# Moving the first five modulation slots behind the first feed-forward layer, and a buffer of its own for one key slot

## The reference, cut to what matters

```python
for i in range(2):                                   # first_block
    x = layer_norm(ALPHA * x + 0.5 * swiglu(x, ffn1...[i]), ...)
    y = mixer_ab(x, ...) if i % 2 == 0 else mixer_c(x, ...)
    x = layer_norm(ALPHA * x + y, ...)
    x = layer_norm(ALPHA * x + 0.5 * swiglu(x, ffn2...[i]), ...)
    x = x + sigmoid(x @ ple_wg[i] + ple_bg[i]) * (p[i] @ ple_wp[i])
for i in range(2):                                   # second_block
    sh1, sc1, g1, sh2, sc2, g2 = split(silu(c) @ w_ada[i] + b_ada[i], 6)   # the modulation
    h = x * (1 + sc1) + sh1
    y, yc = _even_mixer(h, hc, ...) if i % 2 == 0 else _odd_mixer(h, hc, ...)
    x = _layer_norm(ALPHA * x + g1 * y, ...)
    ...
```

## Time and profile before

| what | value |
|---|---|
| median of 3 runs | 2320.36 us (2312.47, 2320.36, 2321.82) |
| profiled execution, its own time | 2311.51 us |
| its span in the profile | 2310.2 us, 39754 instructions |
| mean granted clock of TensorE | 0.991 |
| DVE, ACT busy | 56%, 48% |
| DMA over the span | 353.63 MB, mean 153 GB/s |
| chain that ended last | PE 87%, DVE 6%, ACT 3%, DMA 2%, issue 1% |

### The profile page before, as it was taken

The page is one execution under the profiler, slowest core; times in us unless marked ns, Lnnn a source line. Parts: engine busy times, 40 slices in busy tenths (PEclk is TensorE's granted clock), DMA queues, the critical chain, the costliest instruction groups (busy, mean ns, idle before and its releaser), DMA issues.

```text
span 2310.2 us, 39754 instructions
## 1 busy us (share of the span) xinstructions
PE 2211.9 (96%) x17214; PEld 2003.0 (87%) x17214; DVE 1293.1 (56%) x1953; ACT 1103.0 (48%) x1740; POOL 54.2 (2%) x100
## 2 busy tenths in 40 slices
PE   6999989999999999999999989999999999999998
PEld 5999869999999899979998767888888886778998
DVE  3555756556555766465547326664444564676666
ACT  3444545445544554355445627553333454465554
POOL 1000100000000010010000000000000000000000
PEclk9999999999999999999999999999999999999999
DMA  8444645554545554456453211022222443304451
GB/s 326 183 166 171 259 182 220 186 191 165 190 175 192 205 216 169 159 196 248 166 199 110 91 73 38 20 92 92 91 91 108 166 146 116 122 10 173 170 195 56
DMA packets 52063, 353.63 MB, mean 153 GB/s; under 512 B 8112, under 2 KB 8496, under 8 KB 9392
## 3 DMA queue, kind: packets, MB, share of 16 engines
q1 hardware_dynamic: 47952, 346.05, 39.9%
q10 hardware_dynamic: 864, 4.63, 0.5%
q0 software_dynamic: 3072, 0.40, 0.1%
HBM read 349.61 MB, written 1.05 MB: 152 GB/s over the span
## 4 chain that ended last, share of the span: by engine, by line
PE 87%; DVE 6%; ACT 3%; DMA 2%; issue 1%; SPq 0%; ACTq 0%; DVEq 0%
PE ps L797 14%; PE ps L798 13%; PE ps L799 13%; PE ps L2579 5%; PE ps L2581 5%; PE ps L2580 5%; PE ps L410 2%; PE ps L411 2%; PE ps L412 2%; PE ps L944 2%; PE ps L2332 2%; PE ps L2334 2%; PE ps L2333 2%; DMA ring<-wstream 2%; PE ps L1559 2%; PE ps L1002 1%
## 5 line engine op out<-in xcount | busy, mean ns | idle before, releaser
L385 DVE TENSOR_TENSOR wl<-ring,wh 128x1024 fp32r<-128x1024 f32 x406 | 478.4, 1222 | 274.2 <-ACT wh L380 273.9
L797 PE MATMUL ps<-xs,wh 128*128 128x256 f32 x1760 | 501.4, 285 | 21.7 <-DVE wl L385 8.3
L798 PE MATMUL ps<-xs,wl 128*128 128x256 f32 x1760 | 500.1, 284 | 0.0
L799 PE MATMUL ps<-xs,wh 128*128 128x256 f32 x1760 | 500.0, 284 | 0.0
L380 ACT ACTIVATE wh<-ring 128x1024 fp32r<-128x1024 f32 x406 | 406.1, 1050 | 183.4 <-PE ps L799 128.1
L797 PEld LDWEIGHTS ps<-xs,wh 128*128 128x128 f32 x1760 | 339.9, 193 | 25.5 <-issue 20.5
L799 PEld LDWEIGHTS ps<-xs,wh 128*128 128x128 f32 x1760 | 339.9, 193 | 0.0
L798 PEld LDWEIGHTS ps<-xs,wl 128*128 128x128 f32 x1760 | 339.9, 193 | 0.0
L797 PE MATMUL ps<-hh,wh 128*128 128x256 f32 x880 | 249.1, 283 | 0.7 <-DVE hl L907 0.7
L798 PE MATMUL ps<-hh,wl 128*128 128x256 f32 x880 | 249.0, 283 | 0.0
L799 PE MATMUL ps<-hl,wh 128*128 128x256 f32 x880 | 249.0, 283 | 0.0
(11 more groups left out here) (467 smaller groups left out, 4130.5 us busy)
## 6 DMA issues: line engine op xcount, KB each, us to landing
ring<-wstream SPq DMA_DIRECT2D x329, 1024.0 KB, 4.9
ada_rows<-ada_stage POOLq DMA_DIRECT2D x96, 4.0 KB, 4.8
CN<-consts ACTq DMA_DIRECT2D x1, 1136.0 KB, 15.6
X<-xin ACTq DMA_DIRECT2D x1, 1024.0 KB, 10.6
X<-cin ACTq DMA_DIRECT2D x1, 1024.0 KB, 8.9
out<-X SPq DMA_DIRECT2D x4, 256.0 KB, 2.5
PT__65<-pin ACTq DMA_DIRECT2D x1, 512.0 KB, 18.7
ab_w<-wab ACTq DMA_DIRECT2D x1, 512.0 KB, 3.5
```

Of the source, the lines that this page charges most:

```text
L385: dve.tensor_tensor(lo, tile_of(i), hi.bitcast(F32), ALU.subtract).then_inc(low_part, 1)
L797: pe.matmul(out, wh[:, w, c, :], x_hi, start=start, stop=False, skip_group_check=True)
L798: pe.matmul(out, wl[:, w, c, :], x_hi, start=False, stop=False, skip_group_check=True)
L799: return pe.matmul(out, wh[:, w, c, :], x_lo, start=False, stop=True, skip_group_check=True)
```

## The change

The ada slots' total stays 48. The five at the start go: the stream begins with the first feed-forward layer. One more comes after the last slot of ab_out (TensorE makes it after tile 6), three more into the z tiles of mixer c (after tiles 24, 26 and 28) and one more after c_out's tile 6. All totals of `act_ada` follow. X is loaded by four DMAs of two rows of tiles each, ahead of PV; CN and `pin` are loaded, and `cond` is made, inside the first feed-forward layer after its second hidden tile. The two scaled biases move there too. In the even mixer slot 6 gets a high buffer of its own (`e_wh6`, 8 KB in scratch space), slot 8 waits for slot 4 only, ACT splits slots 7 and 8 together after key tile 1, TensorE puts one rotation behind each of the tiles of slots 5 and 6 but the last, and DVE makes the low parts of 7 and 8 ahead of the last rotation's arithmetic.

```diff
-SECTIONS = ([("ada", 5), ("ffn1_0", 33), ("ada", 1), ("ab_in", 1), ("ada", 3)] + [("ab_in", 1), ("ada", 1)] * 4
-            + [("ab_in", 2), ("alibi", 2)] + [("ab_out", 1), ("ada", 1)] * 4 + [("ffn2_0", 33), ("ple_p_0", 1)]
+SECTIONS = ([("ffn1_0", 33), ("ada", 1), ("ab_in", 1), ("ada", 3)] + [("ab_in", 1), ("ada", 1)] * 4
+            + [("ab_in", 2), ("alibi", 2)] + [("ab_out", 1), ("ada", 1)] * 3 + [("ab_out", 1), ("ada", 2)] + [("ffn2_0", 33), ("ple_p_0", 1)]
...
-            + [x for name, n in (("c_k", 3), ("c_v", 4), ("c_q", 4), ("c_z", 4)) for x in [(name, 1), ("ada", 1)] * n]
-            + [("c_out", 2), ("ada", 3)] + [("c_out", 1), ("ada", 1)] * 2 + [("ada", 1), ("ffn2_1", 33), ("ple_p_1", 1), ("ple_g_1", 4)]
+            + [x for name, n in (("c_k", 3), ("c_v", 4), ("c_q", 4)) for x in [(name, 1), ("ada", 1)] * n]
+            + [("c_z", 1), ("ada", 2)] * 3 + [("c_z", 1), ("ada", 1)]
+            + [("c_out", 2), ("ada", 3)] + [("c_out", 1), ("ada", 1)] * 2 + [("ada", 2), ("ffn2_1", 33), ("ple_p_1", 1), ("ple_g_1", 4)]
...
@@ act_ffn
-                act_xhigh(src)
+                for q in range(4):
+                    c = slice(2 * q, 2 * q + 2)
+                    act.wait_ge(in_x[q], 16)
+                    act.activation(xs[:, c, 0, :], src[:, c, :], ACT.Copy).then_inc(x_high, 1)
...
+                if f == 0 and t == 1:
+                    act.dma_start(CN[:, :], consts).then_inc(in_consts, 16)
+                    act.dma_start(PT_[:, :, :, :], pin).then_inc(in_p, 16)
+                    act.wait_ge(in_params, 16)
+                    act.activation(cond[:, :, :, :], pcol("cond", 0, 16).rearrange("p (c j) -> p c j", j=2).unsqueeze(2)
+                                   .broadcast_to([P, KC, 16, 2]), ACT.Silu).then_inc(cond_ready, 1)
@@ dve_ffn
             if f == 0:
+                for q in range(4):
+                    dve.wait_ge(in_x[q], 16)
                 dve_xlow(name, src)
...
+                if beside and t == 1:
+                    beside()
@@ pe_mixer_ab
-                if n in (1, 3, 5):
+                if n in (1, 3, 5, 6):
                     pe_ada(8)
@@ pe_mixer_c
             tile(24)
+            pe_ada(8)
...
             tile(26)
+            pe_ada(8)
...
             tile(28)
+            pe_ada(8)
...
-                if t in (3, 5):
+                if t in (3, 5, 6):
                     pe_ada(8)
@@ the even mixer
+        e_wh6 = put("e_wh6", [SLOT], F32R, ("hsc", 4096))
...
         def slot_high(s):
-            return e_wh0[:, :] if s == 0 else (e_wh if s < 11 else e_wh2)[:, (s + 1) % 2, :]
+            if s in (0, 6):
+                return (e_wh0 if s == 0 else e_wh6)[:, :]
+            return (e_wh if s < 11 else e_wh2)[:, (s + 1) % 2, :]
...
-            elif s >= 2:
-                before, k = E_SLOTS[s - 2]
+            elif s >= 2 and s != 6:
+                before, k = E_SLOTS[4 if s == 8 else s - 2]
...
+            rotated(0)
+            rotated(1)
...
+            for t in range(4):
                 pe.wait_ge(*e_out.at(f"qB{t}"))
-                pe_slot_tile(6, t % 2, t, hi, lo)
+                pe_slot_tile(5 + t // 2, t % 2, t, hi, lo)
+                if t < 3:
+                    rotated(2 + t)
...
                 act.activation(e_kB[:, t, :], ps[:, t, :], ACT.Copy).then_inc(*e_out(f"kB{t}"))
-                if t % 2:
-                    act_slot_high(7 + t // 2)
+                if t == 1:
+                    act_slot_high(7)
+                    act_slot_high(8)
...
                 if t == 2:
                     dve_slot_low(6)
+                elif t == 4:
+                    dve_slot_low(7)
+                    dve_slot_low(8)
...
-            dve_slot_low(7)
-            dve_slot_low(8)
@@ pe_program, act_program, dve_program
-            pe_ada(40)
-            pe.wait_ge(in_x, 16)
-            pe.wait_ge(in_consts, 16)
-            pe.wait_ge(in_p, 16)
...
                 pe_ffn(2 * i, f"ffn1_{i}")
+                if i == 0:
+                    pe.wait_ge(in_consts, 16)
+                    pe.wait_ge(in_p, 16)
...
-            for s, dst, src in ((in_params, PV[:, :], params), (in_x, X[:, 0, :, :], xin), (in_consts, CN[:, :], consts),
-                                (in_p, PT_[:, :, :, :], pin)):
-                act.dma_start(dst, src).then_inc(s, 16)
...
-            act_ada(40)
-            act.wait_ge(in_x, 16)
+            for q in range(4):
+                act.dma_start(X[:, 0, 2 * q:2 * q + 2, :], xin[:, 2 * q:2 * q + 2, :]).then_inc(in_x[q], 16)
+            act.dma_start(PV[:, :], params).then_inc(in_params, 16)
...
```

More of the change, by code:

```diff
@@ L831, in pe_ffn @@
             gate_up(1)
-            pe.wait_ge(ada_copied, ada["mm"] // KC)
+            if ada["mm"]:
+                pe.wait_ge(ada_copied, ada["mm"] // KC)
             down(0)
@@ L886, in act_ffn, with dve_ffn @@
                     residual(t - 2)
-        def dve_ffn(f, name, src, coef, conv=None, ahead=0, after=()):
+                if f == 0 and t == 1:
[4 more added lines that the diff above has]
+                                   .broadcast_to([P, KC, 16, 2]), ACT.Silu).then_inc(cond_ready, 1)
+        def dve_ffn(f, name, src, coef, conv=None, ahead=0, after=(), beside=None):
             i0 = TILE0[name]
             if f == 0:
+                for q in range(4):
+                    dve.wait_ge(in_x[q], 16)
                 dve_xlow(name, src)
@@ L1980, in act_mixer_c @@
             act_high(t0 + 29)
-            act_ada(296)
+            act_ada(272)
             z_tile(2)
+            act_ada(280)
             act_high(t0 + 30)
@@ L1985, in act_mixer_c @@
             act_high(t0 + 31)
-            act_ada(304)
+            act_ada(288)
             z_tile(4)
+            act_ada(296)
             act.wait_ge(c_att_p, 2)
@@ L2413, in pe_even_mixer, with rotated @@
                 pe_slot_tile(3 + t // 2, t % 2, t, hi, lo)
-            for t in range(5):
+            def rotated(t):
                 q = e_qA[:, t, 0:T] if t < 4 else e_kA[:, 0:T]
@@ L3198, in act_program @@
         def act_program():
-            for s, dst, src in ((in_params, PV[:, :], params), (in_x, X[:, 0, :, :], xin), (in_consts, CN[:, :], consts),
-                                (in_p, PT_[:, :, :, :], pin)):
-                act.dma_start(dst, src).then_inc(s, 16)
-            act.wait_ge(in_params, 16)
-            act.activation(cond[:, :, :, :], pcol("cond", 0, 16).rearrange("p (c j) -> p c j", j=2).unsqueeze(2)
-                           .broadcast_to([P, KC, 16, 2]), ACT.Silu).then_inc(cond_ready, 1)
-            act_ada(40)
-            act.wait_ge(in_x, 16)
+            for q in range(4):
+                act.dma_start(X[:, 0, 2 * q:2 * q + 2, :], xin[:, 2 * q:2 * q + 2, :]).then_inc(in_x[q], 16)
+            act.dma_start(PV[:, :], params).then_inc(in_params, 16)
             act_ffn(0, "ffn1_0", X[:, 0], after=tiles("ab_in"))
             act.wait_ge(eps_set, 3)
-            act_layer_norm("ffn1_0", 64)
+            act_layer_norm("ffn1_0", 24)
             act_mixer_ab()
-            act_layer_norm("ab", 152)
+            act_layer_norm("ab", 120)
             act_ffn(1, "ffn2_0", None, ahead=2, after=tiles("ple_g_0"))
@@ L3214, in act_program @@
             act_ple(0)
-            act_ffn(2, "ffn1_1", X[:, 0], ahead=4, copies=168, after=tiles("c_k"))
-            act_layer_norm("ffn1_1", 192)
+            act_ffn(2, "ffn1_1", X[:, 0], ahead=4, copies=136, after=tiles("c_k"))
+            act_layer_norm("ffn1_1", 160)
             act_mixer_c()
@@ L3241, in dve_program, with scaled_biases @@
             dve.memset(ln_eps[:, 1:2], 1e-6).then_inc(eps_set, 1)
-            dve.wait_ge(in_params, 16)
-            for k, (name, at) in enumerate(LN_AB.values()):
-                dve.tensor_scalar(ln_eps[:, at:at + KC], pcol(LN_GB[name][1], 0, KC), ALPHA, None, ALU.mult
-                                  ).then_inc(eps_set, 1)
-            for s in (in_x, in_consts):
-                dve.wait_ge(s, 16)
+            def scaled_biases():
+                dve.wait_ge(in_params, 16)
+                for name, at in LN_AB.values():
+                    dve.tensor_scalar(ln_eps[:, at:at + KC], pcol(LN_GB[name][1], 0, KC), ALPHA, None, ALU.mult
+                                      ).then_inc(eps_set, 1)
             half = lambda c: 0.5
-            dve_ffn(0, "ffn1_0", X[:, 0], half, after=tiles("ab_in"))
+            dve_ffn(0, "ffn1_0", X[:, 0], half, after=tiles("ab_in"), beside=scaled_biases)
+            dve.wait_ge(in_consts, 16)
             dve_norm_to_parts("ffn1_0")
```

68 lines of the change are left out of this document (33 added, 35 removed).

## The result

| what | before | after |
|---|---|---|
| median of 7 runs each, on one chip | 2315.46 us | 2301.41 us (2298.34 to 2306.78) |
| ratio of the times, 95% interval | | 0.9941 (0.9929 to 0.9953) |
| profiled execution, its own time | 2311.51 us | 2299.87 us |
| its span | 2310.2 us | 2298.6 us |
| mean granted clock of TensorE | 0.991 | 0.993 |

The change makes the kernel faster by 0.59%: 0.0059 x 2315.46 = 13.7 us, with the interval from 10.9 to 16.4. The two profiled executions differ by 11.6. The forecast was 12.7 less, or 2304 us. The prediction took 0.5% for the least that a measurement of this kernel can tell. The interval, 0.47% to 0.71%, reaches across that: the new kernel is faster than the one before, but not clearly by more than 0.5%.

A forecast was written before the change was run, and what follows sets the result against it. TensorE was taken as the bound, its matmuls filling 96% of the span. The terms -10.3 + 0.5 + 5.0 + 1.0 - 8.9 gave -12.7 us, from the runs' mean 2316.5 to 2304; the range ran from 2292 less 2 up to 2313.

The forecast's parts named there:

- Start: Kernel's head: without five ada slots, X is in at 15.5 us and TensorE starts at 20.7 instead of 31.00, -10.3 us.
- turns by packets: Loads at the start: DMA queues alternate by packets, not bytes, so 512 packets of X go beside 512 of the stream.
- slow packets: Rival at the start, chance 0.05: small packets slow the stream to 380 GB/s or below; at most -11.4 us, 2305.
- Clock: First matmuls: TensorE, having done nothing before, runs slow somewhat longer; +0.5 us, between no further loss and 0.9.
- Five ada slots: New places in ab_out, z tiles and c_out: each costs 1.00 us of TensorE, +5.0 us (bounds +3.0 and +8).
- Stream around the layer norms: Behind ab_out and c_out: the next layer's second slot lands later and delays the layer norm, +0.5 us each, +1.0.
- Stream in the z tiles: Mixer c: the changed ring order makes slots z2 and z3 load later, but cover remains, so it costs nothing.
- rival on the slow side: Z tiles and layer norms behind ab_out and c_out: loads land after 10 us instead of 4.9; +12.7 us, 2329, chance 0.06.
- Even mixer: Product with slots 7 and 8: stop gone (-4.8), slow matmuls behind it (-3.0), bunched rotations (-1.1); -8.9 us in all.
- come back in the attention: Rival, chance 0.13: the even mixer's gain is lost again to the attention's first step or the clock; -3.8 us, 2312.7.

The follow-up runs named there:

- e2: The changed kernel without the even mixer's part, so only the new start and the five moved ada slots: 2309.52 us, ratio 0.9984 to the kernel before.
- e5: The changed kernel with one matmul of 8 columns in each of the five moved ada slots: 2298.21 us, ratio 0.9930 to the kernel before.
- e8: The changed kernel with the stream's third slot held until X is in: 2295.20 us, ratio 0.9921 to the kernel before.
- e3: The changed kernel with X loaded by one DMA (8 KB packets) instead of four: 2294.63 us, ratio 0.9914 to the kernel before.
- e7: The changed kernel with slot 8 split behind key tile 3 again and its low part last: 2314.47 us in one execution.
- e1: The kernel before with only the even mixer's part of the change, start and ada slots as before: 2306.98 us, ratio 0.9967 to the kernel before.
- e6: The changed kernel with three rotations together behind key tile 1 and the low parts of slots 7 and 8 last: 2302.38 us in one execution.
- e9: The changed kernel with X in one DMA and the first two weight tiles' splitting put between X's parts: 2291.58 us, ratio 0.9901 to the kernel before.

## Why the prediction came out as it did

- **Start, -10.3 forecast, -8.95 measured.** The mechanism was right at each link: turns by packets (477 and 476), X beside the stream, DVE's 5.04 us behind it. But X was in at 17.0, not 15.5, and two terms of that sum were mis-sized. The rate of 0.42 MB/us held only from 6.5 us on (420 GB/s); the 3.5 us before that had 323, which is 0.34 MB or 0.8 us. And from 3 to 17 us not 5.24 MB went by but 5.54: 4.42 of the stream and 1.12 on X's queue, where the first packets of PV had begun before the last of X were in. That is the other 0.7 us. The rival "slow packets" gave nearly this landing (16.8) and had 0.05, but its mechanism did not come: 2 KB packets beside 8 KB ones kept up 420 GB/s, not 380. Its closeness is chance. Why the first 3.5 us are slower is not shown. It goes with X in four DMAs (323, 312 in e2, 317 in e5, 331 in e8); e3 with one DMA has 410, and the kernel before 415 with PV's packets of 2.5 KB. The estimate from the Trainium skill (DMA: Bandwidth & Descriptors, Measured), 18.4 with its 341 GB/s, was too late by 1.4, the forecast too early by 1.5.
- **Clock, +0.5 forecast, +0.94 measured**, at the edge of the bound (+0.9). The slow steps lasted 5.7 us, where they lasted 3.6 before; 2.2 us more at 0.21 us a step instead of 0.12 are 0.95. But the reason given, a TensorE that has done nothing before, is not borne out: with the same start the slow steps lasted 4.0 us in e2 and 2.9 in e7, and with the old start 6.1 in e1. So this term is not the change's; it is what differs between executions, and that it came out near the forecast is chance. The Trainium skill (TensorE: Matmul & The Clock Gate, What's actually happening) has a start in the throttled state, and the steps of all these executions show it; the granted clock of 1.00 in the window does not. CN, `pin` and `cond` cost nothing, as forecast: 0.93 of the 0.94 is there by the first hidden tile's copy (8.54 us after the first matmul, 7.61 before), ahead of their place.
- **Five ada slots, +5.0 forecast, +5.35 measured.** The three in the z tiles cost 1.00 each, the one behind ab_out 1.18 and the one in c_out 1.17. The row +3.75 of the table is 3.00, 1.17, and -0.42 that lies ahead of z tile 24, where nothing was changed.
- **Stream around the layer norms, +1.0 forecast, nothing measured beyond the slots.** Behind ab_out the weight was late as described, and ended together with TensorE (332.03 and 331.99), so it added nothing in this execution. In e7 it landed later and did. Behind c_out nothing came late.
- **Stream in the z tiles, nothing forecast, nothing measured**: the five steps differ by 1.00 or by nothing. The rival on the slow side asked for landings of 10 us; the median is 4.9 as before.
- **Even mixer, -8.9 forecast, -8.86 measured.** The pieces came out as forecast: the stop 4.81 (4.8), the slow matmuls 2.77 (3.0), the rotations 1.28 (1.1). The tests agree: 8.03 for the late split of slot 8 (e7), 1.26 for the bunching (e6). It did not come back in the attention: e1 keeps it.
- **Not in the sum: where the granted clock falls.** From the first layer norm to that behind ab_out the row is -0.30, though the slot costs 1.18, so 1.48 came from elsewhere. The granted clock from 233 to 253 us was 0.91 before, and 1.00 in the same stretch after. The fall is not the old kernel's own: e6 and e9, which have the change's slots, show it as well (0.95 and 0.91 behind the first layer norm) and take 120.6 and 120.5 us to the next, where the change takes 119.0. The third layer gave 1.36 with no instruction changed (the same stretch takes 230.0 to 233.4 us in the eleven executions), 0.42 came ahead of z tile 24, and behind the attention 3.14 were lost. From the last value tile to the last layer norm but one, the same instructions took 723.8 us before, 726.9 after, and between 725.6 and 730.8 in e1 to e9. In the place that was read closely, it was the granted clock behind a short stop: 1.00 before and 0.83 after in the windows at 1957 and 1945 us. What decides in an execution whether the clock falls there was not found out.

The sum with the measured terms: -8.95 + 0.94 + 5.35 - 8.86 = -11.52, and -0.13 for what belongs to no step, is -11.65, the difference of the two profiled executions. The forecast of -12.7 had 1.35 too much at the start and 0.44 too little for the clock, against 0.65 too much for the slots and the stream around the layer norms (6.0, measured 5.35). The errors partly cancel, and so do the stretches that belong to no step, of 0.4 to 3.1 us each. So the time came out right more closely than its terms.

## What to carry to other kernels

Where DMA queues share the engines by packets, an input that everything waits for should come in packets as large as its neighbour's, or the neighbour should be held back: cutting X into four for an earlier start of the splitting cost 8.1 us of a start that came out at 22.05 and could be 13.95. A stop of TensorE can cost more than its length: 4.8 us of stop cost 7.6 before and 7.9 in e7, with the slow matmuls behind it. Moving the split that it waited for from key tile 3 to key tile 1 was worth all of that. Work taken from the head of a kernel isn't free elsewhere when TensorE is the chain: the five slots took back 5.35 of the 8.95 us, and brought a weight so late that one execution (e7) lost some 3 us by it.

## What was not expected of the hardware

- **X's share of the engines.** 1 MB in packets of 2 KB beside a stream of 8 KB packets took until 17.0 us, in packets of 8 KB until 8.35 (e3), and with the stream held behind its second slot until 11.8 (e8). The rate of both queues together was 420 GB/s from 6.5 us on, not much below the 428 of the earlier trace rows: the loss is X's share, far more than the engines' rate.
- **Eight matmuls for the price of two.** Two of 32 x 256 in one strip of 32 partitions took 1.05 us, eight over four strips 1.00. Leaving out six of the eight gave nothing.
- **The clock's record at the start.** 1.00 from 22 to 26 us beside matmuls at half speed (0.21 us steps, 0.12 from 28 us). Before, the same steps had 0.55 on record, from 31 to 35 us; in e1, with the same start, the record says 1.00 for 31 to 35 us beside the same slow steps. The durations are to be believed.
- **Slow steps of 2.9 to 6.1 us at the start.** The same first matmuls are slow for that long in different executions, with five ada slots ahead of them or none.
- **A free term of some us.** The same work behind the attention took 723.8 to 730.8 us in eleven executions. In the one stop looked at closely, the difference is whether slow clock follows it.
